# Two broadcast rows spread by TensorE, and the final norm's multiplies shared out over ScalarE and GpSimd

## The chip, the cores and the metric

One core of a Trainium2 chip runs the kernel. The metric is the device time of one execution in microseconds (us). Before the change three runs took 2086.59, 2084.54 and 2086.45 us, median 2086.45 us.

## The reference

The program is a two-layer backbone over 512 latent tokens and 256 context tokens of width 1024, all in float32. Layer 0 mixes by retention and a gated linear recurrence, layer 1 by latent attention, and each layer ends in a mixture of 32 experts of which every token uses two. Only the ends of the two expert parts and the final norm matter here:

```python
def rmsnorm(x, g):
    xf = x.astype(jnp.float32)
    y = xf * lax.rsqrt(jnp.mean(xf * xf, axis=-1, keepdims=True) + EPS)
    return (y * g.astype(jnp.float32)).astype(x.dtype)
...
            # layer 0, after the experts: y is the weighed sum of each token's two expert outputs
            xc = xc + mod_c[5] * y[:b * ctx_len].reshape(b, ctx_len, -1)
            xl = xl + mod_l[5] * y[b * ctx_len:].reshape(b, n, -1)
...
            # layer 1
            xl = xl + mod_l[5] * y.reshape(b, n, -1)
    return rmsnorm(xl, final_norm_g)
```

`mod_l[5]` and `mod_c[5]` are rows of 1024 numbers (the gates), `final_norm_g` is another one. The kernel holds tokens on the 128 partitions, so each such row must stand on all 128 partitions before VectorE can multiply a tile by it.

## The kernel before, in words

A tile is 128 tokens by 1024 channels. The token stream `c.X` stays in SBUF (six tiles, the first two are context), and each expert writes its output rows to the DRAM tensor `ys`. Two stages gather them back and are the ones that change.

**The middle stage** is `combine_into_mla` (six tiles; its tiles and semaphores are named `comb_...`, at about 1073 to 1126 us). SP issues three small loads (`laid`, 20 KB in all), then the two gates, each a DMA that copies one DRAM row of 4 KB to all 128 partitions (512 KB written, line 1138), waits until tile 0's gathers have landed, and issues the load of the next stage's weights `w_in` (line 1619, 2688 KB). GpSimd issues per tile two indirect gathers of 512 KB (line 2469). Tile buffers are three deep, so the gather of tile 3 waits until tile 0 is done. ScalarE scales one of the two gathered rows (`weigh`, 2485). VectorE adds the other (2554), multiplies by the gate (2556), adds to `X` (2557). ScalarE squares and sums the tile and takes the root (159, 162), VectorE inverts it (2527), GpSimd refines the inverse by five instructions on one column (2456 to 2460) and scales the identity with it (2463), and TensorE turns the tile with that matrix (2590).

**The last stage** is `combine` (four tiles, from 2042 us to the end). SP loads one gate, waits for tile 0's gathers, loads the final norm's row in the same way (2631), and stores the finished tiles (2637). GpSimd only issues gathers (2357). ScalarE weighs (2373), squares and takes the root. VectorE does the three operations of each tile (2398, 2400, 2401), then, one tile behind, the inverse with its refinement (lines 95 to 100, six small instructions) and the final product with `1/rms` and the norm's row in one instruction (2646). The constant `eps`, which the root needs and for which the first square waits (line 157 and `eps_set`), is set by VectorE after tile 1, in `prepare` (2641).

The order on each engine is the order in which the program lists the instructions; there is no planner. `Chain` makes each linked instruction of an engine wait for the one before it. SP's queue and GpSimd's are in order as well: what stands behind a waiting instruction waits too. In both stages the DMAs of SP and the gathers of GpSimd go to different queues of the same 16 DMA engines.

Of the kernel before, what the change touches and what calls it, by code (L numbers as in the profile page):

```python
# [14 lines left out]
P = 128  # L15
DM = 1024
# [33 lines left out]
class Chain:  # L50


    def __init__(self, eng, sem, base=0):
        self.eng, self.sem, self.n = eng, sem, base
# [117 lines left out]
class NormModulate(RowNorm):  # L172
# [23 lines left out]
    def load(self, sp):  # L196

        self.load_gains(sp)
        self.load_shift_scale(sp)
# [2121 lines left out]
            more.vector(dve)  # L2321


def combine(nc, c, a, layer, t0, r, prefetch=None):


    T = NT - t0
    with Scope(nc, f"comb{layer}") as s:
        YB = 3
        y = [[s.sb(f"y{b}{k}", [P, DM]) for k in range(2)] for b in range(YB)]  # L2330
        got = [s.sem(f"got{b}") for b in range(YB)]
        weighed, x_done, chain = s.sem("weighed"), s.sem("x_done"), s.sem("chain")
        gate = s.sb("gate", [P, 1 if t0 else 2, DM])
        gate_ready = s.sem("gate_ready")
        gs, ex = s.sb("gs", [P, T]), s.sb("ex", [P, T])
        exp_done, w_done = s.sem("exp_done"), s.sem("w_done")
        tile_done = lambda eng, t: eng.wait_ge(x_done, t + 1)
        norm = FinalNorm(nc, c, a, s, t0, tile_done)
        block = s.block()

        @block.sync
        def _(sp):
            load_gates(sp, c, gate, gate_ready, layer, 1, 1 if t0 else 2)
            sp.wait_ge(got[0], 32)
            norm.load(sp)
            if prefetch:
                prefetch(sp)
            norm.store(sp)

        @block.gpsimd  # L2350
        def _(pool):
            for t in range(T + 1):
                if t < T:
                    if t >= YB:
                        pool.wait_ge(x_done, t - YB + 1)
                    for k in range(2):
                        nc.gpsimd.indirect_dma_start(y[t % YB][k][:], None, c.ys[:, :],  # L2357
                                                     bass.IndirectOffsetOnAxis(r.slot[:, k * T + t:k * T + t + 1], 0)
                                                     ).then_inc(got[t % YB], 16)
                if t >= 3:  # L2360
                    norm.shift(pool, t - 3)
            for t in range(T - 2, T):
                norm.shift(pool, t)

        @block.scalar
        def _(act):
            nc.scalar.activation(r.gshift[:, 0:T, :], r.gshift[:, 0:T, :], ACT.Exp).then_inc(exp_done, 1)
            nc.scalar.activation(ex[:], r.eshift[:, 0:T], ACT.Exp).then_inc(exp_done, 1)
            act.wait_ge(w_done, 1)
            for t in range(T + 2):  # L2370
                if t < T:
                    act.wait_ge(got[t % YB], 32 * (t // YB + 1))
                    nc.scalar.mul(y[t % YB][0][:], y[t % YB][0][:], r.w[:, 0, t:t + 1]).then_inc(weighed, 1)  # L2373
                if 1 <= t <= T:
                    norm.square(act, t - 1)
                if t >= 2:
                    norm.first_half(act, t - 2)
                    norm.second_half(act, t - 2, nc.scalar.copy)

        @block.vector  # L2380
        def _(dve):
            link = Chain(dve, chain)
            V = nc.vector


            dve.wait_ge(exp_done, 2)
# [5 lines left out]
            dve.wait_ge(gate_ready, 16 if t0 else 32)  # L2392
            for t in range(T + 2):
                if t < T:
                    st = 1 if t0 + t < CT else 0
                    y0, y1 = y[t % YB]
                    dve.wait_ge(weighed, t + 1)
                    link(V.scalar_tensor_tensor(out=y0[:], in0=y1[:], scalar=r.w[:, 1, t:t + 1], in1=y0[:],  # L2398
                                                op0=ALU.mult, op1=ALU.add))
                    link(V.tensor_tensor(y0[:], y0[:], gate[:, st, :], ALU.mult))  # L2400
                    V.tensor_tensor(c.X[:, t0 + t, :], c.X[:, t0 + t, :], y0[:], ALU.add).then_inc(x_done, 1)  # L2401
                if t == 1:
                    norm.prepare(dve)
                if 1 <= t <= T:
                    norm.scale(dve, link, t - 1)

        @block.tensor
        def _(pe):
            for t in range(T):
                norm.transpose(pe, t)  # L2410


def combine_into_mla(nc, c, a, r, m):
# [4 lines left out]
    with Scope(nc, f"comb{layer}") as s:  # L2418
        YB = 3
        y = [[s.sb(f"y{b}{k}", [P, DM]) for k in range(2)] for b in range(YB)]  # L2420
        got = [s.sem(f"got{b}") for b in range(YB)]
        gate = s.sb("gate", [P, 2, DM])
        gs, ex = s.sb("gs", [P, T]), s.sb("ex", [P, T])
        turn = [s.sb(f"turn{i}", [P, P]) for i in range(2)]
        laid = s.sb("laid", [5 * KD, P])
# [5 lines left out]
        (gate_ready, weighed, x_done, chain, exp_done, w_done, laid_ready, cols_tr, cols_done, rstd_done, scaled, tr, ev_act,  # L2431
         ev_dve, pchain, inverted, kv_done, kv_out) = (s.sem(n) for n in (
             "gate_ready", "weighed", "x_done", "chain", "exp_done", "w_done", "laid_ready", "cols_tr", "cols_done",
             "rstd_done", "scaled", "tr", "ev_act", "ev_dve", "pchain", "inverted", "kv_done", "kv_out"))
        norm = RowNorm(nc, c, a, s, 0, lambda eng, t: eng.wait_ge(x_done, t + 1), s.sb)
        block = s.block()
# [41 lines left out]
        def _(act):  # L2478
            nc.scalar.activation(r.gshift[:, 0:T, :], r.gshift[:, 0:T, :], ACT.Exp).then_inc(exp_done, 1)
            nc.scalar.activation(ex[:], r.eshift[:, 0:T], ACT.Exp).then_inc(exp_done, 1)  # L2480
            act.wait_ge(w_done, 1)

            def weigh(t):
# [35 lines left out]
        def _(dve):  # L2519
# [97 lines left out]

class Box:
    pass


class FinalNorm(RowNorm):


    def __init__(self, nc, c, a, s, t0, x_ready):
        super().__init__(nc, c, a, s, t0, x_ready, s.sb)
        self.o = s.sb("o", [P, self.T, DM])
        self.o_done, self.stored = s.sem("o_done"), s.sem("stored")

    def load(self, sp):  # L2630
        sp.dma_start(self.g[:], self.a["final_norm_g"].rearrange("(o n) -> o n", o=1)
                     .to_broadcast([P, DM])).then_inc(self.g_ready, 16)

    def store(self, sp):
        for t in range(self.T):
            sp.wait_ge(self.o_done, t + 1)
            sp.dma_start(self.c.out[0, t * P:(t + 1) * P, :], self.o[:, t, :]).then_inc(self.stored, 16)
        sp.wait_ge(self.stored, 16 * self.T)

    def prepare(self, dve):  # L2640
        self.nc.vector.memset(self.eps[:], EPS).then_inc(self.eps_set, 1)
        dve.wait_ge(self.g_ready, 16)

    def scale(self, dve, link, t):
        self.inverse(dve, link, t)
        self.nc.vector.scalar_tensor_tensor(out=self.o[:, t, :], in0=self.c.X[:, self.t0 + t, :],  # L2646
                                            scalar=self.rstd[:, t:t + 1], in1=self.g[:],
                                            op0=ALU.mult, op1=ALU.mult).then_inc(self.o_done, 1)

    def shift(self, pool, t):  # L2650
        pass

    transpose = first_half = shift

    def second_half(self, eng, t, copy):
        pass


def backbone(nc, a, out):
# [71 lines left out]
```

## Time and profile before

| | us |
|---|---|
| median of three runs | 2086.45 |
| the profiled execution, time | 2084.73 |
| its span, first to last instruction | 2083.1 |
| TensorE busy | 1703.4 (82%) |
| VectorE busy | 691.1 (33%) |
| ScalarE busy | 439.0 (21%) |
| GpSimd busy | 257.6 (12%) |

The span is what the trace shows. The 1.6 us between span and time lie before and behind it. A share of busy time is an average over stages with different limits. The chain of waits is followed back from the last instruction only as far as 2042 us, that is over the last stage.

### The profile page before, as it was taken

How to read it: one execution, taken by the hardware profiler on the slowest of the kernel's cores; microseconds unless marked ns; L12 is line 12 of the kernel's file. 1: busy time of each engine (PE TensorE's matmuls, PEld its weight loads, DVE VectorE, ACT ScalarE, POOL GpSimd, SP SyncE). 2: the span in 40 equal slices, each digit the busy share in tenths (PEclk: the TensorE clock that was granted, in tenths of full speed). 3: DMA queues.
4: the chain of work that ended last, by engine and by line, in shares of the span. 5: the costliest groups of instructions: out<-in, count | busy, mean ns of one | idle time of the engine just before them, and what ended most of it. 6: DMA issues, size and time to landing. Idle time of an engine off the chain costs nothing. (4 is left out here: it accounts for less than half of the span.)

```text
span 2083.1 us, 26474 instructions
## 1 busy us (share of the span) xinstructions
PE 1703.4 (82%) x9120; PEld 884.2 (42%) x9121; DVE 691.1 (33%) x1241; ACT 439.0 (21%) x842; POOL 257.6 (12%) x381
## 2 busy tenths in 40 slices
PE   5999999799499789997638999999948899766560
PEld 3443344645245334443316445555534344333330
DVE  3404675733312111111124447775432111111114
ACT  3103454211001100111124125553101101101012
POOL 1002440311101000101013200000121000000001
PEclk9999999899599899999778999999959899877775
DMA  9876744410789999999972102001459999999994
GB/s 371 270 265 222 278 161 153 170 82 31 303 335 398 415 417 409 420 413 407 424 278 91 59 0 92 1 1 50 176 223 394 418 406 414 419 416 424 419 387 148
DMA packets 98212, 560.19 MB, mean 269 GB/s; under 512 B 17188, under 2 KB 35328, under 8 KB 58584
## 3 DMA queue, kind: packets, MB, share of 16 engines
q1 hardware_dynamic: 85104, 522.39, 63.1%
q0 software_dynamic: 7744, 20.98, 3.0%
q10 hardware_dynamic: 5288, 15.80, 2.0%
q8 instruction: 48, 0.79, 0.2%
q14 instruction: 28, 0.23, 0.0%
HBM read 522.88 MB, written 41.50 MB: 271 GB/s over the span
## 5 line engine op out<-in xcount | busy, mean ns | idle before, releaser
L2136 PE MATMUL exp_gps<-moew_wg,all_hT 128*64 128x512 f32 (+1 forms) x480 | 248.3, 643 | 48.2 <-DMA moew_wu<-in_moe_w_up 42.5
L2130 PE MATMUL exp_gps<-moew_wg,all_hT 128*32 128x256 f32 x1088 | 167.5, 475 | 130.9 <-DMA moew_wu<-in_moe_w_up 123.2
L2137 PE MATMUL exp_ups<-moew_wu,all_hT 128*64 128x512 f32 (+1 forms) x480 | 246.1, 638 | 0.0
L588 PE MATMUL abp_ps<-ab_w,all_hT 128*128 128x512 f32 x384 | 169.8, 597 | 0.6 <-PE abp_ps L592 0.3
L2130 PE MATMUL exp_ups<-moew_wu,all_hT 128*32 128x256 f32 x1088 | 166.7, 474 | 1.5 <-issue 1.5
L2130 PEld LDWEIGHTS exp_gps<-moew_wg,all_hT 128*32 128x32 f32 x1088 | 74.5, 135 | 195.7 <-issue 173.8
L2136 PEld LDWEIGHTS exp_gps<-moew_wg,all_hT 128*64 128x64 f32 (+1 forms) x480 | 79.8, 171 | 171.5 <-issue 170.5
L2278 DVE TENSOR_TENSOR all_hT<-all_hT,exp_ups 64x512 f32<-64x512 f32 (+1 forms) x30 | 20.7, 690 | 370.4 <-ACT all_hT L2221 370.4
L2177 PE MATMUL exp_yps<-moew_wd,all_hT 128*64 128x512 f32 (+1 forms) x240 | 115.1, 596 | 0.0
L2179 PE MATMUL exp_yps<-moew_wd,all_hT 128*64 128x512 f32 (+1 forms) x240 | 115.1, 596 | 0.0
L588 PEld LDWEIGHTS abp_ps<-ab_w,all_hT 128*128 128x128 f32 x384 | 71.4, 190 | 99.0 <-issue 97.5
L2276 DVE TENSOR_TENSOR all_hT<-all_hT,exp_ups 64x256 f32<-64x256 f32 x34 | 14.4, 424 | 290.2 <-ACT all_hT L2219 290.2
L2137 PEld LDWEIGHTS exp_ups<-moew_wu,all_hT 128*64 128x64 f32 (+1 forms) x480 | 80.6, 171 | 54.5 <-issue 54.5
L2089 POOL COPY exp_idx<-all_tok 128x1 int32 (+1 forms) x64 | 11.5, 180 | 743.4 <-DVEq L2267 699.8
L1432 PE MATMUL att_sc<-mlakv_KT,mlak_QT 96*128 96x384 f32 x256 | 100.4, 517 | 1.7 <-PEq L76 1.7
L2221 ACT ACTIVATE all_hT<-exp_gps 64x512 f32<-64x512 f32 (+1 forms) x30 | 17.8, 592 | 363.6 <-PE exp_ups L2137 363.6
L592 PE MATMUL abp_ps<-all_hT,ab_w 128*128 128x256 f32 (+1 forms) x256 | 87.8, 500 | 2.0 <-DVE all_hT L745 1.7
L2114 PE MATMUL exp_xps<-all_ident,all_hT 128*128 128x128 f32 x512 | 74.5, 290 | 14.0 <-DMA all_hT<-h_rows,exp_idx 14.0
L2114 PEld LDWEIGHTS exp_xps<-all_ident,all_hT 128*128 128x128 f32 x512 | 64.3, 194 | 47.4 <-issue 47.4
L1504 DVE TENSOR_REDUCE att_nmax<-att_sc 128x1 f32<-128x768 f32 x64 | 61.2, 956 | 49.6 <-PE att_sc L1432 49.6
L2130 PEld LDWEIGHTS exp_ups<-moew_wu,all_hT 128*32 128x32 f32 x1088 | 73.7, 135 | 4.9 <-issue 2.0
L2219 ACT ACTIVATE all_hT<-exp_gps 64x256 f32<-64x256 f32 x34 | 12.8, 375 | 292.3 <-PE exp_ups L2130 292.3
(425 smaller groups left out, 2531.2 us busy)
## 6 DMA issues: line engine op xcount, KB each, us to landing
moew_wg<-in_moe_w_gate SPq DMA_DIRECT2D x64, 2048.0 KB, 29.5
moew_wu<-in_moe_w_up SPq DMA_DIRECT2D x64, 2048.0 KB, 38.2
moew_wd<-in_moe_w_down SPq DMA_DIRECT2D x64, 2048.0 KB, 33.4
all_X<-in_ada_w SPq DMA_DIRECT2D x40, 1024.0 KB, 8.0
ab_w<-in_ab_w_in SPq DMA_DIRECT2D x6, 2048.0 KB, 9.1
ys<-abp_zero SPq DMA_DIRECT2D x32, 384.0 KB, 8.4
ys<-exp_y ACTq DMA_DIRECT2D x13, 512.0 KB, 10.1
ab_rows<-in_ada_w SPq DMA_DIRECT2D x6, 1024.0 KB, 16.1
```

What stands on the lines that cost most here:

```text
L588: last = nc.tensor.matmul(ps[i % RB][:], hT[:, kk, what * P:(what + 1) * P], w[n % S][:, kk, :], start=(kk == 0), stop=(kk == KD - 1))
L592: last = nc.tensor.matmul(ps[i % RB][:, 0:m], w[n % S][:, kk, ct * P:(ct + 1) * P], hT[:, kk, o:o + m], start=(kk == 0), stop=(kk == KD - 1))
L1432: last = nc.tensor.matmul(sc[n % 2][:, b, 0:HALF], k.QT[0:QD, h, t * P:(t + 1) * P], k.KT[0:QD, h, b * HALF:(b + 1) * HALF], start=True, s ...
L1504: V.tensor_reduce(nmax[:, n % R:n % R + 1], sc[n % 2][:, :, 0:HALF], mybir.AxisListType.XY, ALU.max, negate=True).then_inc(mx, 1)
L2114: last = nc.tensor.transpose(xps[k // 4][:, k % 4, :], x_by[q][:, k, :], c.ident[:])
L2130: last = nc.tensor.matmul(bank[lo + j * Q:lo + (j + 1) * Q, 0:HC], x[:, k, 0:Q], wt[:, k, j * HC:(j + 1) * HC], start=(k == 0), stop=(k == ...
L2136: nc.tensor.matmul(gps[0:rows, :], x[:, k, 0:rows], w.g[q][:, k, :], start=(k == 0), stop=(k == KD - 1))
L2137: last = nc.tensor.matmul(ups[at:at + rows, :], x[:, k, 0:rows], w.u[q][:, k, :], start=(k == 0), stop=(k == KD - 1))
L2177: nc.tensor.matmul(yps[0][0:rows, :], hT[:, k, 0:rows], w.d[q][:, k, 0:512], start=(k == 0), stop=(k == HT_N - 1))
L2179: last = nc.tensor.matmul(yps[1][at:at + rows, :], hT[:, k, 0:rows], w.d[q][:, k, 512:1024], start=(k == 0), stop=(k == HT_N - 1))
L2221: nc.scalar.activation(sg[at:at + rows, :], gps[0:rows, :], ACT.Silu).then_inc(sg_done, 1)
L2278: nc.vector.tensor_tensor(h[at:at + rows, :], sg[at:at + rows, :], ups[at:at + rows, :], ALU.mult).then_inc(h_done, 1)
```

## The change

In both stages the gate rows are loaded as they are, 4 KB to one partition. TensorE multiplies a column of ones by that row, four times 512 numbers, which puts the row on all 128 partitions in PSUM. ScalarE copies the first half of each 1024 numbers to SBUF, VectorE the second. In the last stage the second row spread this way is the final norm's. In the middle stage both are gates, and the PSUM banks used are those that later take the turned tiles.

In the last stage the final norm is shared out anew. VectorE sets `eps` first and keeps only the reciprocal. GpSimd refines the inverse behind the last gather. For tiles 0 to 2 ScalarE multiplies the tile by `1/rms`, and GpSimd multiplies it by the norm's row. Tile 3 is finished by VectorE in one instruction as before. `FinalNorm` goes.

```diff
+def load_gate_rows(sp, c, row, ready, layer, sub, streams):
+    for st in range(streams):
+        sp.dma_start(row[0:1, st * DM:(st + 1) * DM],
+                     c.mods[st, layer:layer + 1, (sub * 3 + 2) * DM:(sub * 3 + 3) * DM]).then_inc(ready, 16)
...
 def combine(nc, c, a, layer, t0, r):                                  # last stage
         def _(sp):
-            load_gates(sp, c, gate, gate_ready, layer, 1, 1 if t0 else 2)
-            sp.wait_ge(got[0], 32)
-            norm.load(sp)
+            load_gate_rows(sp, c, row, row_ready, layer, 1, 1)
+            sp.dma_start(row[0:1, DM:], a["final_norm_g"].rearrange("(o n) -> o n", o=1)).then_inc(row_ready, 16)
+            for t in range(T):
+                if t < T - 1:
+                    sp.wait_ge(o_done, t + 1)
+                else:
+                    sp.wait_ge(last_done, 1)
+                sp.dma_start(c.out[0, t * P:(t + 1) * P, :], o[:, t, :]).then_inc(stored, 16)
...
         def _(pool):
+            def refine(t):
+                col = slice(t, t + 1)
+                pool.wait_ge(inverted, t + 1)
+                link(nc.gpsimd.tensor_scalar(ms[:, col], ms[:, col], 1.0 / DM, EPS, ALU.mult, ALU.add))
+                link(nc.gpsimd.tensor_tensor(tmp[:, col], rstd[:, col], rstd[:, col], ALU.mult))
+                link(nc.gpsimd.tensor_tensor(tmp[:, col], tmp[:, col], ms[:, col], ALU.mult))
+                link(nc.gpsimd.tensor_scalar(tmp[:, col], tmp[:, col], -0.5, 1.5, ALU.mult, ALU.add))
+                nc.gpsimd.tensor_tensor(rstd[:, col], rstd[:, col], tmp[:, col], ALU.mult).then_inc(refined, 1)
+            def gained(t):
+                pool.wait_ge(spread_act, 2)
+                pool.wait_ge(spread_dve, 2)
+                pool.wait_ge(scaled, t + 1)
+                nc.gpsimd.tensor_tensor(o[:, t, :], o[:, t, :], gain, ALU.mult).then_inc(o_done, 1)
+            for t in range(T):
                 ...                                                   # all gathers as before
+            for t in range(T):
+                refine(t)
+                if t < T - 1:
+                    gained(t)
...
         def _(act):
+            for i in range(0, 4, 2):
+                act.wait_ge(spread_done, i + 1)
+                nc.scalar.copy(spread[:, i // 2, 0:512], bps[i][:]).then_inc(spread_act, 1)
...
+            def scale(t):
+                act.wait_ge(refined, t + 1)
+                nc.scalar.mul(o[:, t, :], c.X[:, t0 + t, :], rstd[:, t:t + 1]).then_inc(scaled, 1)
+            weigh(0)
+            weigh(1)
+            act.wait_ge(eps_set, 1)
+            for t in range(T):
+                square(t)
+                if t + 2 < T:
+                    weigh(t + 2)
+                if 1 <= t < T:
+                    scale(t - 1)
...
         def _(dve):
+            V.memset(eps[:], EPS).then_inc(eps_set, 1)
...
+            for i in range(1, 4, 2):
+                dve.wait_ge(spread_done, i + 1)
+                V.tensor_copy(spread[:, i // 2, 512:], bps[i][:]).then_inc(spread_dve, 1)
+            dve.wait_ge(spread_act, 2)
+            dve.wait_ge(spread_dve, 2)
+            for t in range(T):
                 ...                                                   # the three operations of a tile as before
+                if t >= 1:
+                    inverse(t - 1)                                    # waits root_done, one reciprocal
+            inverse(T - 1)
+            dve.wait_ge(refined, T)
+            V.scalar_tensor_tensor(out=o[:, T - 1, :], in0=c.X[:, t0 + T - 1, :], scalar=rstd[:, T - 1:T], in1=gain,
+                                   op0=ALU.mult, op1=ALU.mult).then_inc(last_done, 1)
...
         def _(pe):
+            pe.wait_ge(row_ready, 32)
+            for i in range(4):
+                nc.tensor.matmul(bps[i][:], c.ones[0:1, :], row[0:1, i * 512:(i + 1) * 512], start=True, stop=True).then_inc(spread_done, 1)
...
 def combine_into_mla(nc, c, a, r, m):                                 # middle stage
-            load_gates(sp, c, gate, gate_ready, layer, 1, 2)
+            load_gate_rows(sp, c, row, row_ready, layer, 1, 2)
             sp.wait_ge(got[0], 32)
             load_w_in(sp, a, m)
...
+            # ScalarE, behind its two exponentials: banks 0 and 2; VectorE, behind cols: banks 1 and 3
+                nc.scalar.copy(gate[:, i // 2, 0:512], tp[i][:].rearrange("p a b -> p (a b)")).then_inc(spread_act, 1)
+                V.tensor_copy(gate[:, i // 2, 512:], tp[i][:].rearrange("p a b -> p (a b)")).then_inc(spread_dve, 1)
-            dve.wait_ge(gate_ready, 32)
+            dve.wait_ge(spread_act, 2)
+            dve.wait_ge(spread_dve, 2)
...
+            # TensorE, behind the transpose of laid
+            pe.wait_ge(row_ready, 32)
+            for i in range(4):
+                nc.tensor.matmul(tp[i][:].rearrange("p a b -> p (a b)"), c.ones[0:1, :], row[0:1, i * 512:(i + 1) * 512],
+                                 start=True, stop=True).then_inc(spread_done, 1)
```

## Rows read from the trace of the kernel before

**Rows 1.** Page, costliest groups: mean ns of one, then idle time before them.
```profile
L2130 PE MATMUL exp_gps<-moew_wg,all_hT 128*32 128x256 f32 x1088 | 167.5, 475 | 130.9 <-DMA moew_wu<-in_moe_w_up 123.2
```
**Rows 2.** Chain of waits, last stage: start us, us, what.
```profile
2044.39 5.66 DMA comb_y<-ys,all_slot
...
2051.43 1.30 DVE comb_y L2398
...
2055.24 1.21 DVE comb_y L2398
...
2077.51 1.28 DVE comb_o L2646
```
**Rows 3.** Timeline, last stage: start us, us, engine, line, operation.
```profile
2042.40 0.35 SPq L1138 DMA_DIRECT2D comb_gate<-mods  x1
2043.11 0.97 POOL L2357 DMA_INDIRECT comb_y<-ys,all_slot  x1 [70.96 <-PEq L73]
...
2055.51 1.75 POOL L2357 DMA_INDIRECT comb_y<-ys,all_slot  x1 [5.17 <-DVE all_X L2401]
...
2059.01 1.06 ACT L159 ACTIVATE comb_njunk<-all_X 128x1024 f32<-128x1024 f32 x1 [4.46 <-DVE comb_neps L2641]
...
2061.67 1.13 ACT L2373 ACTIVATE comb_y<-comb_y,all_w 128x1024 f32<-128x1024 f32 x1
```
**Rows 4.** Timeline, middle stage.
```profile
1073.61 0.38 SPq L2443 DMA_DIRECT2D comb_laid<-in_norm_g  x1
1074.03 0.82 SPq L1138 DMA_DIRECT2D comb_gate<-mods  x2
...
1075.15 0.33 PE L2569 MATMUL comb_cps<-all_ident,comb_laid 40*128 40x40 f32 x1 [7.11 <-DMA comb_laid<-in_norm_g]
...
1084.54 1.28 DVE L2554 SCALAR_TENSOR_TENSOR comb_y<-comb_y,all_w 128x1024 f32<-128x1024 f32 x1 [8.55 <-ACT comb_y L2485]
...
1097.76 1.15 ACT L2485 ACTIVATE comb_y<-comb_y,all_w 128x1024 f32<-128x1024 f32 x1 [4.16 <-DMA comb_y<-ys,all_slot]
...
1102.26 1.27 DVE L2554 SCALAR_TENSOR_TENSOR comb_y<-comb_y,all_w 128x1024 f32<-128x1024 f32 x1
```
**Rows 5.** Windows from tile 0's first gather to its landing: busy times, TensorE clock, DMA share, GB/s.
```profile
1073.48:1083.17 9.69, 0.33 (x1) 0.18 (x1) 1.14 (x7) 0.88 (x3) 5.71 (x6) 0.50 0.85 274
2043.11:2050.05 6.94, 0.00 (x0) 0.00 (x0) 0.67 (x4) 0.90 (x3) 5.41 (x6) 0.50 0.84 270
```
**Rows 6.** Tile view of the middle stage's gates: us from issue to landing.
```profile
DMA to landing us min/median/max: 5.0/6.6/8.3
```
**Rows 7.** Window of TensorE at half clock, six matmuls of 128x512 (columns as in rows 5).
```profile
560.70:565.80 5.10, 5.10 (x6) 2.13 (x7) 0.00 (x0) 1.00 (x1) 1.04 (x1) 0.50 0.95 382
```
**Rows 8.** Timeline of the same place: two such matmuls, one behind the other.
```profile
562.51 1.92 PE L2137 MATMUL exp_ups<-moew_wu,all_hT 128*128 128x512 f32 x2
```
**Rows 9.** Groups by shape: copies of one PSUM bank, mean ns.
```profile
L2211 ACT COPY all_hT<-exp_xps 128x512 f32<-128x512 f32 x64 | 37.4, 585 | 114.7 <-PE exp_xps L2114 114.7
L2268 DVE COPY all_hT<-exp_xps 128x512 f32<-128x512 f32 x64 | 44.1, 690 | 26.5 <-PE exp_xps L2114 25.8
```
**Rows 10.** Timeline of GpSimd in the middle stage, VectorE busy, then idle.
```profile
1092.22 0.19 POOL L2456 TENSOR_SCALAR comb_nms<-comb_nms 128x1 f32<-128x1 f32 x1 [0.61 <-DVE comb_nrstd L2527]
1092.49 1.11 POOL L2457 TENSOR_TENSOR comb_ntmp<-comb_nrstd 128x1 f32<-128x1 f32 x1
...
1096.20 0.19 POOL L2460 TENSOR_TENSOR comb_nrstd<-comb_nrstd,comb_ntmp 128x1 f32<-128x1 f32 x1
...
1099.60 0.19 POOL L2456 TENSOR_SCALAR comb_nms<-comb_nms 128x1 f32<-128x1 f32 x1
...
1100.70 0.19 POOL L2460 TENSOR_TENSOR comb_nrstd<-comb_nrstd,comb_ntmp 128x1 f32<-128x1 f32 x1
```
**Rows 11.** Timeline, attention's output stage: GpSimd and VectorE at once.
```profile
1466.99 2.35 POOL L277 TENSOR_TENSOR mlak_QT<-mlak_QT 128x1024 f32<-128x1024 f32 x1 [290.11 <-DVE mlak_QT L268]
...
1467.74 2.14 DVE L1132 TENSOR_TENSOR all_X<-all_X,mla_cqT 128x512 f32<-128x512 f32 x1
```

More of the change, by code:

```diff
@@ L2331, in combine @@
         got = [s.sem(f"got{b}") for b in range(YB)]
-        weighed, x_done, chain = s.sem("weighed"), s.sem("x_done"), s.sem("chain")
-        gate = s.sb("gate", [P, 1 if t0 else 2, DM])
-        gate_ready = s.sem("gate_ready")
-        gs, ex = s.sb("gs", [P, T]), s.sb("ex", [P, T])
-        exp_done, w_done = s.sem("exp_done"), s.sem("w_done")
-        tile_done = lambda eng, t: eng.wait_ge(x_done, t + 1)
-        norm = FinalNorm(nc, c, a, s, t0, tile_done)
+        o, junk = s.sb("o", [P, T, DM]), s.sb("junk", [P, DM])
+        row = s.sb("row", [1, 2 * DM])
+        spread = s.sb("spread", [P, 2, DM])
+        gate, gain = spread[:, 0, :], spread[:, 1, :]
+        bps = [s.ps(f"bps{i}", [P, 512]) for i in range(4)]
+        gs, ex = s.sb("gs", [P, T]), s.sb("ex", [P, T])
+        ms, root, rstd, tmp = (s.sb(n, [P, T]) for n in ("ms", "root", "rstd", "tmp"))
+        eps = s.sb("eps", [P, 1])
+        (weighed, x_done, chain, pchain, row_ready, spread_done, spread_act, spread_dve, exp_done, w_done, eps_set, sq, root_done,
+         inverted, refined, scaled, o_done, last_done, stored) = (s.sem(n) for n in (
+             "weighed", "x_done", "chain", "pchain", "row_ready", "spread_done", "spread_act", "spread_dve", "exp_done", "w_done",
+             "eps_set", "sq", "root_done", "inverted", "refined", "scaled", "o_done", "last_done", "stored"))
         block = s.block()
@@ L2350, in _ @@
+            sp.wait_ge(stored, 16 * T)
         @block.gpsimd
         def _(pool):
[L2352 to L2361, printed above, removed]
@@ L2362, in _ @@
-            for t in range(T - 2, T):
-                norm.shift(pool, t)
+            link = Chain(pool, pchain)
+            def refine(t):
[6 more added lines that the diff above has]
+                nc.gpsimd.tensor_tensor(rstd[:, col], rstd[:, col], tmp[:, col], ALU.mult).then_inc(refined, 1)
@@ new lines, in gained @@
+            def gained(t):
[4 more added lines that the diff above has]
+            for t in range(T):
+                if t >= YB:
+                    pool.wait_ge(x_done, t - YB + 1)
+                for k in range(2):
+                    nc.gpsimd.indirect_dma_start(y[t % YB][k][:], None, c.ys[:, :],
+                                                 bass.IndirectOffsetOnAxis(r.slot[:, k * T + t:k * T + t + 1], 0)
+                                                 ).then_inc(got[t % YB], 16)
@@ L2368, in _, with weigh, square @@
             nc.scalar.activation(ex[:], r.eshift[:, 0:T], ACT.Exp).then_inc(exp_done, 1)
+            for i in range(0, 4, 2):
+                act.wait_ge(spread_done, i + 1)
+                nc.scalar.copy(spread[:, i // 2, 0:512], bps[i][:]).then_inc(spread_act, 1)
             act.wait_ge(w_done, 1)
[L2370 to L2378, printed above, removed]
+            def weigh(t):
+                act.wait_ge(got[t % YB], 32 * (t // YB + 1))
+                nc.scalar.mul(y[t % YB][0][:], y[t % YB][0][:], r.w[:, 0, t:t + 1]).then_inc(weighed, 1)
+            def square(t):
+                col = slice(t, t + 1)
+                act.wait_ge(x_done, t + 1)
+                nc.scalar.activation(junk[:], c.X[:, t0 + t, :], ACT.Square, accum_out=ms[:, col]).then_inc(sq, 1)
+                act.wait_ge(sq, t + 1)
+                nc.scalar.activation(root[:, col], ms[:, col], ACT.Sqrt, scale=1.0 / DM, bias=eps[:]).then_inc(root_done, 1)
+            def scale(t):
[10 more added lines that the diff above has]
+                    scale(t - 1)
         @block.vector
@@ L2390, in _ @@
             V.tensor_tensor(r.w[:, 1, 0:T], r.w[:, 0, 0:T], ex[:], ALU.mult).then_inc(w_done, 1)
+            for i in range(1, 4, 2):
+                dve.wait_ge(spread_done, i + 1)
+                V.tensor_copy(spread[:, i // 2, 512:], bps[i][:]).then_inc(spread_dve, 1)
             dve.wait_ge(w_done, 1)
[L2392 to L2405, printed above, removed]
+            dve.wait_ge(spread_act, 2)
+            dve.wait_ge(spread_dve, 2)
+            for t in range(T):
+                y0, y1 = y[t % YB]
+                dve.wait_ge(weighed, t + 1)
+                link(V.scalar_tensor_tensor(out=y0[:], in0=y1[:], scalar=r.w[:, 1, t:t + 1], in1=y0[:],
+                                            op0=ALU.mult, op1=ALU.add))
+                link(V.tensor_tensor(y0[:], y0[:], gate, ALU.mult))
+                V.tensor_tensor(c.X[:, t0 + t, :], c.X[:, t0 + t, :], y0[:], ALU.add).then_inc(x_done, 1)
+                if t >= 1:
[4 more added lines that the diff above has]
+                                   op0=ALU.mult, op1=ALU.mult).then_inc(last_done, 1)
         @block.tensor
         def _(pe):
-            for t in range(T):
-                norm.transpose(pe, t)
+            pe.wait_ge(row_ready, 32)
+            for i in range(4):
+                nc.tensor.matmul(bps[i][:], c.ones[0:1, :], row[0:1, i * 512:(i + 1) * 512], start=True, stop=True).then_inc(spread_done, 1)
 def combine_into_mla(nc, c, a, r, m):
@@ L2422, in combine_into_mla @@
         gate = s.sb("gate", [P, 2, DM])
+        row = s.sb("row", [1, 2 * DM])
         gs, ex = s.sb("gs", [P, T]), s.sb("ex", [P, T])
@@ L2480, in _ @@
             nc.scalar.activation(ex[:], r.eshift[:, 0:T], ACT.Exp).then_inc(exp_done, 1)
+            for i in range(0, 4, 2):
+                act.wait_ge(spread_done, i + 1)
+                nc.scalar.copy(gate[:, i // 2, 0:512], tp[i][:].rearrange("p a b -> p (a b)")).then_inc(spread_act, 1)
             act.wait_ge(w_done, 1)
@@ L2619 @@
     pass
[L2622 to L2656, printed above, removed]
 def backbone(nc, a, out):
```

14 lines of the change are left out of this document (8 added, 6 removed).

## The prediction

> **What bounds the kernel now.** I read the page first. TensorE is busy for most of the span, and its largest group stood idle for 131 us, 123 of them waiting for expert weights [rows 1]. The change touches neither. It touches two short stages between the bulk parts, where everything hangs on the gathers of tile 0. So I read the chain of waits next, then the timeline of each stage. In the last stage the chain goes through the landing of tile 0's gathers (2044.39 + 5.66 = 2050.05 us), then VectorE, which starts at 2051.43 and ends its last instruction at 2078.79 [rows 2]. I call that start S; before, the end is S + 27.4. In the middle stage VectorE starts at 1084.54, 1.37 us after the landing at 1083.17 [rows 4, 5]. All later work of that stage and of the program follows in order from this start, and no transfer of the next part runs ahead of it except `w_in`, so I take a microsecond won there as a microsecond of the program.
>
> **Middle stage, what goes.** Two gates, 2 x 128 rows of 4 KB = 1.05 MB, leave the DMA engines. Up to the landing they moved 274 GB/s x 9.69 us = 2.66 MB, in the last stage, with one gate, 270 x 6.94 = 1.87 MB [rows 5]. Without gates 1.61 MB are left, at 274 GB/s 5.9 us, so tile 0 lands at 1073.48 + 5.9 = 1079.4. That keeps the share of tile 1 that moved along. Bounds: 6.9 us as with one gate (1080.4), and 3.9 us for the 1.05 MB of tile 0 alone (1077.4).
>
> **Middle stage, what comes.** The nearest small load, `laid`'s third, was issued at 1073.61, and TensorE started on it at 1075.15, 1.54 us later. The two row loads stand where the gates stood, so the second goes out at 1074.44 [rows 4] and has landed at 1076.0. The slower bound is 5.0 us, the fastest landing of a gate [rows 6]; I take 1.54, since the bytes (4 KB) are those of that load. TensorE's clock was granted at 0.50 here, its 1.2 GHz level, after tens of us with next to no matmul [rows 5]. At 0.50 a 128x512 matmul takes 0.85 us (5.10 / 6) and the last of a run 1.92 - 0.85 = 1.07 [rows 7, 8]. The four end at 1077.1, 1077.9, 1078.8 and 1079.6. ScalarE copies banks 0 and 2 (0.585 us each) and is free at 1079.4, VectorE banks 1 and 3 (0.69) and is done at 1080.4 [rows 9]. Behind these copies stand ScalarE's `weigh(0)` and VectorE's tile 0. ScalarE is free just when the tile lands, and its scaling covers VectorE's last copy: VectorE starts at 1079.4 + 1.37 = 1080.8. That is **3.8 us** early. If the tile lands sooner ScalarE's copies hold it and nothing more is won; at 1080.4 it is 2.8. The cover is thin: a row landing 1 us later costs 0.6 to 1 us.
>
> The small instructions of GpSimd and the PSUM banks are first needed more than 10 us later, so the spread delays nothing there. `w_in` is issued at the landing and moves with it.
>
> **Last stage, start.** One gate, 0.52 MB, goes, and the norm's row, which competed with tiles 1 and 2. 1.87 - 0.52 = 1.35 MB at 270 GB/s is 5.0 us. The other estimate is tile 3, gathered alone: at most 2061.67 - 2055.51 = 6.2 us, of which 0.8 is its slower first issue (1.75 against 0.97) [rows 3], so 5.4. I take 5.2: landed at 2048.3. The second row load is issued at 2042.75 and lands at 2044.3; the matmuls end from 2045.4 to 2047.9; ScalarE is free at 2047.7, VectorE at 2048.7. Hidden. VectorE starts at 2048.3 + 1.38 = 2049.7, **1.7 us** early. Bounds 0 (nothing comes of the bytes) and 2.4 (ScalarE's copies hold it).
>
> The DMA engines serve both queues at once in these rows. By the Trainium skill, "DMA: Bandwidth & Descriptors", section "SWDGE vs HWDGE vs iDMA", each engine takes turns between the two kinds of queue; a gate would then cost the gathers its own bytes, 1.9 us, where the rows with one and two gates differ by 2.75. By that difference tile 0 would land 0.8 us sooner in the last stage.
>
> **Last stage, the rest,** in us from S. A tile costs VectorE 2055.24 - 2051.43 = 3.8 [rows 2]. What goes is its wait for `eps` and the root (2.9 between tiles 1 and 2), five small refinements and one 1.3 us product per tile, except the last. Left to itself VectorE would be done with tile 3 at about 15.7. So the end is set elsewhere:
> - Tile 0 done 3.8. ScalarE's square, table load, root take 2061.67 - 2059.01 = 2.7 [rows 3]: root at 6.6, `weigh(2)` to 7.8. VectorE ends tile 1 at 7.6, inverts, starts tile 2 at 7.85, ends at 11.65.
> - GpSimd refines tile 0 from 7.9. While VectorE works, one column takes it 1.11 instead of 0.19: from 1092.22 to 1096.39, 4.2 us in all; idle, 1099.60 to 1100.89, 1.3, with the hand-over 1.4 [rows 10]. Refined at 12.05. Meanwhile ScalarE waits for tile 3 (at most 10.3) and weighs it, then scales tile 0 from 12.1 to 13.25 (1.15, as `weigh`).
> - GpSimd's product of 128x1024 took 2.35 us [rows 11]. In that time VectorE's sum of two SBUF tiles, 128x512, took 2.14, where one twice as wide takes 1.30 [rows 2]: it was held until GpSimd was done. So `gained(0)` asks at 13.35, gets the port at 14.45 behind VectorE's product and ends at 16.8; VectorE's last sum for tile 3 stands until then and ends at 17.95; refinement of tile 1 ends at 19.15.
> - From here VectorE is idle and GpSimd and ScalarE take turns, since `gained(t)` stands before `refine(t + 1)` in GpSimd's queue: scale(1) 20.4, gained(1) 22.8, refine(2) 24.2, scale(2) 25.4, gained(2) 27.85, refine(3) 29.25, VectorE's last product 30.6.
>
> 30.6 - 27.4 = **3.2 us** late. The stores are as many and as large as before, the last alone. Bounds: without any holding VectorE ends tile 3 at 15.65, gained(0) ends at 15.7, and the rest of the chain, refine 1.4, scale 1.2, gained 2.4 twice and refine and product, 2.8, ends at 28.5: + 1.1. Upwards, one more VectorE operation in the way of GpSimd: + 4.5.
>
> The row shows the holding. The Trainium skill, "SBUF — State Buffer", section "SBUF: two separate sides", says that a GpSimd operation and a VectorE operation with two SBUF inputs exclude each other for a whole instruction, whoever comes first; that speaks against giving GpSimd wide products beside VectorE. Its absence would be the + 1.1 above.
>
> **Sum.** - 3.8 - 1.7 + 3.2 = - 2.3 us. Against the profiled execution: 2084.73 - 2.3 = 2082.4. That execution was 1.7 below the median of the three runs, whose own spread is 2; taken off the median 2086.45, the forecast is **2084.2 us**. 0.2% is 4.2 us, about what a measurement of this kernel can tell from no change.
>
> **Rivals.**
> - *Both starts at their best and no holding* (faster): - 3.8 - 2.4 + 1.1 = - 5.1, 2081.3 us. For it: the difference of 2.75 us per gate. Against: the held sum [rows 11].
> - *The middle gain is given back* (same): `w_in`, 2.75 MB, now starts 3.8 us sooner and meets the gathers of tiles 1 and 2 still in the queue, so these land late. For it: up to now they had a head start, and tile 3's `weigh` at 1097.76 did wait for DMA. Against: that tile was used only at 1102.26, 3.3 us after it was weighed [rows 4], and 1 MB less is to be moved. Price about 2 us: - 0.3, 2086.2 us.
> - *The rows land late* (slower): one mechanism, the landing of the row loads. If they take 5.0 us [rows 6], the middle stage's second lands at 1079.4, the matmuls end at 1083.1, VectorE's copy at 1083.8, and it starts at about 1084.2, a gain of 0.3. In the last stage the row lands at 2047.8, ScalarE is free at 2051.2, VectorE starts at 2052.5, 1.1 late. With + 3.2 that is + 4.0, with a tail at its upper bound + 5.3: 2090.5 to 2091.8 us. It starts to cost once the rows take over 1.6 us in the middle stage and 2.1 in the last, and with 3.2 in both the change is worth nothing. Against: `laid`'s 1.54.
>
> **How the numbers follow.** Forecast 0.64, its own range - 4 to 0 (2082.4 to 2086.5). At its best 0.14, given back 0.14, rows late 0.06, something else 0.02. The range runs from the best case less 0.8 of scatter to the given-back case plus 1.8: 2080.5 to 2088.0. Faster by over 0.2% needs 4.2 us: the best case and an edge of the forecast, 0.16. Slower by over 0.2%: 0.06. Same: 0.78.
>
> **What would show it.** Right: VectorE's first three-step tile starts 5.9 + 1.4 = 7.3 us after the first gather's issue in the middle stage instead of 11.1, and 6.6 instead of 8.3 in the last; TensorE's four spread matmuls at 0.50 end before the gathers land; a VectorE sum of about 3.5 us for tile 3; last product some 30.6 after S. Wrong: spread matmuls waiting past the landing; tiles 1 or 2 late behind `w_in`; GpSimd's products well off 2.35; or the bulk parts between the stages longer or shorter by over 1 us.

## The result: 0.18% slower, and where

Over 20 runs each, the changed kernel takes 2092.16 us in the median against 2087.97 before; the ratio of the means is 1.0018 with a 95% interval of 1.0010 to 1.0027, that is + 3.8 us (+ 2.1 to + 5.6). The forecast was - 2.3 us, its range ended at 2088.0. Single runs of either kernel scatter over some 10 us (before 2080.7 to 2094.0, changed 2086.5 to 2096.2), so I read the stages in the traces, each counted from its own first gather. Up to the middle stage the two programs are the same, and yet the two profiled executions reach it at 1073.5 and 1078.8 us. So 5.3 of the 10 us between the two spans (2083.1 and 2093.2) lie ahead of the first changed instruction.

**The middle stage after.** The timeline, in the columns of [rows 4]:

```profile
1078.78 0.97 POOL L2529 DMA_INDIRECT comb_y<-ys,all_slot  x1 [70.09 <-POOLq L76]
...
1079.32 0.51 SPq L2327 DMA_DIRECT2D comb_row<-mods  x2
...
1082.21 7.19 PE L2639 MATMUL comb_tp<-comb_row,all_ones 1*128 1x512 f32 x8 [1.58 <-DMA comb_row<-mods]
...
1085.27 0.40 SPq L1619 DMA_DIRECT2D mlakv_V<-in_mla_w_in  x1
...
1089.43 0.69 DVE L2614 COPY comb_gate<-comb_tp 128x512 f32<-128x512 f32 x1 [2.62 <-PE comb_tp L2639]
1090.23 1.28 DVE L2621 SCALAR_TENSOR_TENSOR comb_y<-comb_y,all_w 128x1024 f32<-128x1024 f32 x1
```

`w_in` goes out at the landing of tile 0, 6.5 us after the first gather instead of 9.7 [rows 5]: the gathers gained 3.2 us. VectorE starts 11.45 us after the first gather, 0.4 later than before (11.06). In between stands TensorE: four instructions, **eight** records in the trace, 7.19 us.

**The last stage after.** The chain of waits now goes through TensorE at the start, and through GpSimd and ScalarE in turn to the end; where [rows 2] have the landing of the gathers, it has the spread:

```profile
2050.24 7.20 PE comb_bps L2469 x8
2057.47 0.70 DVE comb_spread L2447
...
2058.39 1.30 DVE comb_y L2454
...
2069.83 1.15 ACT comb_y L2407
2070.98 1.05 ACT comb_o L2418
...
2072.19 2.34 POOL comb_o L2382
...
2077.78 1.16 ACT comb_o L2418
...
2079.09 2.34 POOL comb_o L2382
...
2082.84 1.16 ACT comb_o L2418
...
2084.15 2.34 POOL comb_o L2382
...
2087.89 1.28 DVE comb_o L2462
```

VectorE starts 9.21 us after the first gather (2049.18) instead of 8.32, and from there to the end of its last product is 30.78 us instead of 27.36. The three together: + 0.4 + 0.9 + 3.4 = + 4.7 us, inside the interval. This trace has 1.7 us more inside the middle stage, which come from TensorE's clock and not from the change (see e7 and e8 below).

### The profile page after: what moved, and what is told of

It reads as the page before. It is cut to its first block and busy times, and to the rows that moved or that the text cites. A ratio compares the mean times of both kernels' runs of the same rounds, so it can differ in the third digit from the quotient of the medians.

```text
span 2093.2 us, 26520 instructions
## 1 busy us (share of the span) xinstructions
PE 1715.6 (82%) x9136; PEld 877.1 (42%) x9137; DVE 689.5 (33%) x1222; ACT 444.0 (21%) x849; POOL 273.1 (13%) x404
## 5 line engine op out<-in xcount | busy, mean ns | idle before, releaser
L2094 POOL DMA_INDIRECT all_hT<-h_rows,exp_idx x64 | 62.9, 982 | 92.2 <-issue 92.2
```

The lines of the kernel that those rows point to most:

```text
L2094: nc.gpsimd.indirect_dma_start(xg[q][0:rows, :], None, c.h_rows[:, :], bass.IndirectOffsetOnAxis(idx[q][0:rows, :], 0), bounds_check=TOK - ...
```

## The experiments

For each kernel the starts of VectorE after the stage's first gather, the end of TensorE's last latent matmul in the middle stage likewise, and the tail (VectorE's first three-step operation to its last product), all from the timelines of the profiled executions. There is one trace of each kernel. Where a stage is the same word for word, the traces differ by 0.1 us in the middle start with the spread (11.39 to 11.49), by 0.2 without it (10.84 to 11.06), and by 0.2 in the last start (8.32 to 8.55, 9.20 to 9.36):

| kernel | middle start | middle end | last start | tail | ratio to before (95%) |
|---|---|---|---|---|---|
| before | 11.06 | 63.8 | 8.32 | 27.36 | |
| changed | 11.45 | 65.5 | 9.21 | 30.78 | 1.0018 (1.0010 to 1.0027) |
| e1, half spread | 8.14 | 60.9 | 8.00 | 30.41 | 1.0011 (1.0000 to 1.0021), not comparable |
| e2, spread, old tail | 11.48 | 64.1 | 9.36 | 27.27 | 0.9998 (0.9988 to 1.0008) |
| e3, old rows, new tail | 10.87 | 63.6 | 8.32 | 30.64 | 1.0011 (1.0000 to 1.0023) |
| e4, refine first | 11.49 | 64.2 | 9.28 | 26.99 | 1.0003 (0.9993 to 1.0013) |
| e5, gain after x | 11.39 | 64.1 | 9.20 | 31.35 | one execution |
| e6, early eps | 10.84 | 63.6 | 8.38 | 24.34 | 0.9984 (0.9975 to 0.9994) |
| e7, needed row first | 8.18 | 63.1 | 7.84 | 30.98 | 1.0006 (0.9997 to 1.0015) |
| e8, that and e6 | 8.29 | 62.9 | 8.48 | 24.94 | 0.9977 (0.9965 to 0.9990) |
| e9, e8, gathers apart | 8.04 | 66.8 | 7.99 | 27.35 | one execution |
| e10, old rows, VectorE tail | 10.84 | 65.3 | 8.55 | 22.45 | 0.9977 (0.9966 to 0.9987) |
| e11, spread and VectorE tail | 8.08 | 61.6 | 7.96 | 22.27 | 0.9952 (0.9939 to 0.9965) |

**e1: is it the spread that holds the starts?**

```diff
-nc.tensor.matmul(bps[i][:], c.ones[0:1, :], row[0:1, i * 512:(i + 1) * 512], ...)
+nc.tensor.matmul(bps[i][:, 0:256], c.ones[0:1, :], row[0:1, i * 512:i * 512 + 256], ...)   # both stages
```

> The changed kernel, but each of the four spread matmuls of both stages covers 256 of its 512 numbers; the copies read these twice, so the second half of each row is wrong. Theory (the spread is what holds the starts): at half clock the four matmuls take 3.6 us instead of 7.2, the price that the prediction had put on the whole spread, so VectorE's first operation comes 7.9 us after the first gather's issue in the middle stage (11.45 in the changed kernel, 11.06 before) and about 6.8 in the last (9.21 and 8.32); the tail of the last stage stays at 30.8 us; the time falls by some 6 us against the changed kernel, 2 against the one before. Rival (the gathers land no sooner without the gates): both starts stay within 0.5 us of before, 11 and 8.3.

Its tile view has the records of the matmuls of each stage, minimum, median and maximum in ns:

```profile
L2639 PE MATMUL comb_tp<-comb_row,all_ones x8: 629/629/791, 1080.1 to 1083.3; 1*128 1x256 f32 x8
```

The changed kernel's view has the same eight at twice the width:

```profile
L2639 PE MATMUL comb_tp<-comb_row,all_ones x8: 1056/1056/1215, 1082.2 to 1088.3; 1*128 1x512 f32 x8
```

The spread takes 3.78 us, the middle stage starts at 8.14 and ends 2.9 us sooner than before. So the gathers do land sooner, and the spread was in the way. In the last stage the start is 8.00: only 0.3 better than before, and not the 6.8 expected. There the spread is over 5.0 us after the first gather, and in its timeline ScalarE still waits for the gathers until 6.7:

```profile
2051.76 0.69 DVE L2447 COPY comb_spread<-comb_bps 128x512 f32<-128x512 f32 x1 [1.01 <-PE comb_bps L2469]
2053.45 1.15 ACT L2407 ACTIVATE comb_y<-comb_y,all_w 128x1024 f32<-128x1024 f32 x1 [1.96 <-DMA comb_y<-ys,all_slot]
```

Its time was expected 2 us below before's and came out 2.3 us above (0 to 4.4), where its stages in the table give - 0.2. The likely reason is that wrong gates in layer 0 send tokens to other experts in layer 1, but no run shows that, so e1 counts here for its two stages and not for its total.

**e2 and e3: one half of the change each.** e2 keeps the spread and has VectorE's refinement and products back (`link(V.reciprocal(...))` to the product, `eps` set after tile 1); e3 is the kernel before with the new tail.

> The changed kernel with the old sharing of the final norm: eps set after tile 1, refinement and last product of every tile on VectorE. Theory: starts as in the changed kernel (11.45 and 9.2 us after the first gather's issue), the last stage's tail from VectorE's first operation back from 30.8 to 27.4 us; against before about +1.3 us. Rival (the late start itself stretches the tail, since tile 3's gather comes later relative to the rest): the tail stays above 29.

> The kernel before with only the new sharing of the final norm; all rows are loaded by the broadcast DMAs as before. Theory: starts as before (11.06 and 8.3 us after the first gather's issue), tail 30.8 us instead of 27.4; against before about +3.4 us. Rival (the tail is long only because the late spread shifts ScalarE and GpSimd against VectorE): the tail is at most 28.5, about +1 us.

Both stages and tails came out by the theory: 11.48, 9.36 and 27.27; 10.87, 8.32 and 30.64. By the traces the two halves add up, neither needs the other, and the tail is the dearer one (+ 3.3). The two ratios agree with that (e2 + 1.4 us by its stages, e3 + 3.1), but are too wide to show it alone.

**e5: is it the hold between VectorE and GpSimd?**

```diff
             for t in range(T):
                 refine(t)
+                if t == 0:
+                    pool.wait_ge(x_done, T)
                 if t < T - 1:
                     gained(t)
```

> The changed kernel, but GpSimd's first wide product also waits until VectorE has added tile 3, so the two never hold each other. Theory (the turns of GpSimd and ScalarE behind one another set the end): VectorE's product for tile 3 falls from 3.28 to 1.22 us and tile 3 is ready 2 us sooner, but the tail stays within 0.6 us of 30.8. Rival (the held VectorE is what costs): the tail falls by the 2 us to about 28.7.

In the changed kernel's timeline the first wide product of GpSimd meets VectorE's gate product of tile 3, which takes 3.28 us instead of 1.22:

```profile
2072.19 2.34 POOL L2382 TENSOR_TENSOR comb_o<-comb_o,comb_spread 128x1024 f32<-128x1024 f32 x1 [1.94 <-ACT comb_o L2418]
2072.33 3.28 DVE L2456 TENSOR_TENSOR comb_y<-comb_y,comb_spread 128x1024 f32<-128x1024 f32 x1
```

In e5's timeline the same VectorE product is free, and GpSimd follows:

```profile
2068.79 1.22 DVE L2458 TENSOR_TENSOR comb_y<-comb_y,comb_spread 128x1024 f32<-128x1024 f32 x1
2070.05 1.22 DVE L2459 TENSOR_TENSOR all_X<-all_X,comb_y 128x1024 f32<-128x1024 f32 x1
2071.35 2.34 POOL L2382 TENSOR_TENSOR comb_o<-comb_o,comb_spread 128x1024 f32<-128x1024 f32 x1 [4.35 <-DVE all_X L2459]
```

Tile 3 is done 2.3 us sooner (16.1 instead of 18.5 from VectorE's start), the tail is 31.35. The hold is real, and waiting it out gains nothing: GpSimd's first product now starts 16.2 us after VectorE's start instead of 13.8. What the tail would be if neither engine held the other, no run here shows.

**e4: is it the order in GpSimd's queue?**

```diff
-            for t in range(T):
-                refine(t)
-                if t < T - 1:
-                    gained(t)
+            refine(0)
+            for t in range(1, T):
+                refine(t)
+                gained(t - 1)
```

> The changed kernel; in GpSimd's queue of the last stage the refinement of tile t + 1 stands before the wide product of tile t. Theory (the order in GpSimd's queue makes refinement, ScalarE's scaling and the wide product take turns): ScalarE's scaling of tile 2 and VectorE's last product no longer wait for wide products in front of their refinement; the tail falls from 30.8 to about 27 us, with the starts unchanged (11.45 and 9.2). VectorE's operations are held as before. Rival (GpSimd's total work sets the end, in whatever order): three wide products and four refinements are the same, the tail stays above 29.5.

26.99. With the same instructions, 3.8 us are gone; GpSimd's total work is not the bound. VectorE was still held, in tile 3's sum (3.39 us) and, as its timeline shows, in the last product, behind `gained(2)`:

```profile
2080.51 2.34 POOL L2382 TENSOR_TENSOR comb_o<-comb_o,comb_spread 128x1024 f32<-128x1024 f32 x1
2080.59 3.33 DVE L2462 SCALAR_TENSOR_TENSOR comb_o<-all_X,comb_rstd,comb_spread 128x1024 f32<-128x1024 f32 x1 [3.44 <-POOL comb_rstd L2376]
```

**e6: what was there to win with the smallest edit?**

```diff
 # combine, VectorE, first instruction
+            V.memset(norm.eps[:], EPS).then_inc(norm.eps_set, 1)
 # FinalNorm.prepare
-        self.nc.vector.memset(self.eps[:], EPS).then_inc(self.eps_set, 1)
```

> The kernel before; only eps is set at the start of the last stage instead of after tile 1. Theory: VectorE's wait of 2.9 us for the first root goes and nothing takes its place; the tail falls from 27.4 to 24.5 us, starts as before (11.06 and 8.3); about -2.9 us against before. Rival (tile 3's gather is late next and holds VectorE): 1 to 2 us are given back, tail 26.

24.34: the tail alone is 3.0 us shorter, and the time is 3.3 us (1.3 to 5.2) below before's.

**e7 and e8: the row that is needed first, first.**

```diff
-            for i in range(4):
+            for i in (2, 3, 0, 1):       # middle stage: the context gate first
...
             weigh(0)
             weigh(1)
+            spread_half(3, 0)            # ScalarE's half of the other row; VectorE's stands behind tile 0
```

> The changed kernel; the row that is needed first is spread first (context gate in the middle stage, the gate in the last), and the copies of the other row stand behind the second weighing on ScalarE and behind tile 0 on VectorE. Theory: only 3.6 us of TensorE stand before the first tile, so VectorE starts 7.8 us after the first gather's issue in the middle stage and 8.0 in the last, where now the landing of the gathers holds it; tail 30.7. About -0.5 us against before, -5 against the changed kernel. Rival (the other row's copies hold tile 0 or 1 anyway): the starts are early, but tile 1 starts over 4.5 us behind tile 0.

> The needed row spread first, as in the run beside it, with the old sharing of the final norm and eps set at the start. Theory: the two starts at 7.8 and 8.0 us, the tail 24.5: -3.2 - 0.3 - 2.9 = -6.4 us against before, ratio 0.9969. Rival (the middle stage's gain is given back by late gathers of tiles 2 and 3): tile 5 of the middle stage starts 40.4 us after the first gather as before instead of 37.2, and the total is only about -3 us.

The starts came (8.18 and 7.84), e7's time stayed level with before (1.0006), and e8's fell by 4.8 us (2.1 to 7.3) where 6.4 were expected. e8's last start is 8.48, no better than before's: its gathers landed late, ScalarE started on them 7.2 us after the first. The middle stage's end gained only 0.7 and 0.9 of the 2.8 us. Two things show. VectorE's late copy puts tile 1 at 4.33 instead of 3.7 behind tile 0, as e7's timeline shows:

```profile
1085.19 1.28 DVE L2638 SCALAR_TENSOR_TENSOR comb_y<-comb_y,all_w 128x1024 f32<-128x1024 f32 x1
...
1088.91 0.68 DVE L2624 COPY comb_gate<-comb_tp 128x512 f32<-128x512 f32 x1
...
1089.52 1.27 DVE L2638 SCALAR_TENSOR_TENSOR comb_y<-comb_y,all_w 128x1024 f32<-128x1024 f32 x1
```

And the first group of latent matmuls (eight instructions, sixteen records) took 5.81 us where it took 4.12 before, which moves the rest by 1.7. That is TensorE's clock, and the spread does not decide it: e10, whose middle stage is the old one word for word, has the slow group, while e3 and e6, equally old there, have not; the changed kernel's trace has it, while e2, e4 and e5, with the same middle stage word for word, have not. The first fence is e10's timeline, the second e3's.

```profile
1109.69 5.81 PE L2620 MATMUL comb_kps<-mlakv_V,all_hT 128*128 128x288 f32 x16 [2.89 <-issue]
```

```profile
1108.87 4.12 PE L2617 MATMUL comb_kps<-mlakv_V,all_hT 128*128 128x288 f32 x16 [2.84 <-issue]
```

The changed kernel's own 65.5 holds 1.7 us of it. Windows over that group give the granted clock as the third number from the end, 0.71 in the changed kernel,

```profile
1111.90:1117.80 5.90, 5.85 (x18) 4.41 (x19) 4.92 (x8) 4.75 (x9) 4.22 (x10) 0.71 0.18 67
```

and 1.00, the 2.4 GHz level, before:

```profile
1106.60:1110.80 4.20, 4.15 (x18) 3.34 (x19) 4.13 (x6) 3.29 (x7) 3.36 (x5) 1.00 0.24 91
```

What sets the two kinds of trace apart stands just before the group, in the turnings of tiles 0 and 1. Here is the changed kernel's timeline:

```profile
1102.86 3.74 PE L2661 MATMUL comb_tp<-comb_turn,all_X 128*128 128x128 f32 x16 [13.46 <-POOL comb_turn L2523]
1107.36 2.05 PE L2661 MATMUL comb_tp<-comb_turn,all_X 128*128 128x128 f32 x16 [0.76 <-POOL comb_turn L2523]
1111.95 5.81 PE L2650 MATMUL comb_kps<-mlakv_V,all_hT 128*128 128x288 f32 x16 [2.54 <-issue]
```

The clock had risen to 1.00 before the first turning was over, the second took 2.05 us instead of 3.78, TensorE idled for 2.54 us, and in the group the clock was back at 0.50 from about 1113.2 to 1116.6. In the five traces with the slow group (changed, e7, e8, e10, e11) the first turning takes 3.40 to 3.74 us. In the other eight it takes 3.78 or 3.79, so there the clock rose later, and it stayed at 1.00 through the group. Why it rose sooner in some stays open.

**e9: why does tile 0 land no sooner than 6.5 us?**

```diff
             for t in range(T):
+                if t == 1:
+                    pool.wait_ge(got[0], 32)
```

> The version with the needed row spread first and the old sharing of the norm; GpSimd issues tile 1's and tile 2's gathers only when tile 0 has landed, in both stages. Theory (tile 0's 1 MB lands late, 6.4 to 6.9 us after the first issue, since the gathers behind it take part of the DMA engines): it lands at about 5.3, so ScalarE's first weighing in the last stage starts at 5.4 instead of 7.0, and w_in goes out at 5.3 instead of 6.5. Rival (that time belongs to two gathers of random rows, whatever stands behind them): both stay within 0.3 us of 6.5. Tiles 1 and 2 land late in either case, so the total says nothing.

The rival came true. With nothing behind them, tile 0's gathers land after 6.49 us in the middle stage and ScalarE starts on them at 6.69 in the last, by the timeline:

```profile
2049.73 0.97 POOL L2372 DMA_INDIRECT comb_y<-ys,all_slot  x1 [68.10 <-POOLq L76]
2051.01 0.96 POOL L2372 DMA_INDIRECT comb_y<-ys,all_slot  x1 [0.31 <-issue]
2056.42 1.15 ACT L2389 ACTIVATE comb_y<-comb_y,all_w 128x1024 f32<-128x1024 f32 x1 [2.89 <-DMA comb_y<-ys,all_slot]
```

**e10 and e11: a version that beats both.** GpSimd only refines tiles 0 to 2, ScalarE scales nothing, and VectorE makes the products when its three-step work is over, filling with two of them the time in which ScalarE squares tile 3. e11 adds the spread, the needed row first, the other row's copies both on ScalarE.

```diff
+            for t in range(T - 1):                       # GpSimd, behind the gathers
+                refine(t)
...
+            def finish(t):                               # VectorE
+                if t < T - 1:
+                    dve.wait_ge(refined, t + 1)
+                else:
+                    ...                                  # root_done, refined_rsqrt on VectorE
+                V.scalar_tensor_tensor(out=o[:, t, :], in0=c.X[:, t0 + t, :], scalar=rstd[:, t:t + 1], in1=gain,
+                                       op0=ALU.mult, op1=ALU.mult).then_inc(o_done, 1)
+            for t in (0, 1, 3, 2):
+                finish(t)
```

> The kernel before with only the last stage's norm changed: eps at the start, GpSimd refines tiles 0 to 2 behind the last gather, and VectorE makes all last products, those of tiles 0 and 1 while ScalarE squares tile 3, then tile 3's refinement and product, then tile 2's; ScalarE scales nothing. Theory (what made the new tail long is that ScalarE's and GpSimd's wide operations take turns, not the moving of small ones): tail 22.2 us, starts as before; -5.2 us against before, ratio 0.9975. Rival (GpSimd, blocked by VectorE's wide operations, refines too late): tail 24.5 or more.

> The same last stage with the rows spread by TensorE, the needed one first, and the second row's copies both on ScalarE behind its second weighing. Theory: middle stage starts at 8.2 us, tile 1 follows 3.8 behind tile 0 and the stage ends 2.8 us earlier than before (61.0 instead of 63.8 us after the first gather, if the clock rises as it did there), last stage starts at 8.0, tail 22.2: -2.8 - 0.3 - 5.2 = -8.3 us against before, ratio 0.996. Rival (of the spread's gain nothing arrives behind the middle stage): as the run beside it, ratio 0.9975.

The tails are 22.45 and 22.27. e11 takes 2079.67 us against 2089.67 for the kernel before beside it, ratio 0.9952 (0.9939 to 0.9965). The stages give - 2.2 (middle, with the slow clock in its profile), - 0.4 and - 5.1 = - 7.7 us; the interval runs from - 7.3 to - 12.7. e10, measured beside it with the old rows and the same tail, has a median of 2084.87. So the spread, with only the needed row ahead of tile 0, is worth some 5 us; the stages of the two traces, which both have the slow group, give 3.7 + 0.6 + 0.2 = 4.5. e11 is also the only kernel but e9 in which VectorE waited for tile 2 of the middle stage (0.92 us), since ScalarE's weighing waited for that tile's gathers; whether `w_in`, which was in transfer then, held them up, no run shows.

## Why the prediction was wrong

- **The step that failed is the price of the spread**: "At 0.50 a 128x512 matmul takes 0.85 us (5.10 / 6)". I divided by records. The float32 matmuls of these stages leave two records for each instruction, as the eight for four instructions above show, so one costs 1.7 to 1.8 us and the four 7.2, not 3.6. The timeline of before could have told: tile 0's turning, eight matmuls in the program, stands there as sixteen (only the 40x40 transpose of `laid` leaves one):

```profile
1097.16 3.78 PE L2590 MATMUL comb_tp<-comb_turn,all_X 128*128 128x128 f32 x16 [21.68 <-POOL comb_turn L2463]
```

  e1, which pays about the price I had written down (3.78 us), says how much this is: with it the middle stage is at - 2.9 and the last at - 0.3, with the full price at + 0.4 and + 0.9. So the price moved the two starts by 3.3 and 1.2, together 4.5 of the 7.0 us that lie between the forecast of - 2.3 and the + 4.7 of the stages. What the next two points say is nearly all of the rest, 0.9 and 1.4 us.
- **The gathers' landing in the middle stage** was sized at 5.9 us and measured 6.2 to 6.9 (6.5 in the changed kernel and in e1): 0.6 of the 3.8 were too much. The late rows below make up the rest of the way from - 3.8 to e1's - 2.9.
- **In the last stage** it was sized at 5.2. Where the spread is out of the way, ScalarE starts on the gathers 6.7 us after the first in e1, e9 and e11, 6.6 in e7 and 7.2 in e8, against 7.0 to 7.3 in the traces with the broadcast gate (before, e3, e6, e10). One gate fewer brought some 0.3 us, not 1.7. Bytes over rate was the wrong model, since 0.52 MB fewer should have saved 1.9 by it. Why one gate costs some 0.3 us in the last stage and two cost 3 in the middle (6.5 without, 9.5 to 9.7 with) stays open; e9 only shows that, with no gate in the queues, the 6.5 us do not come from the gathers behind.
- **The tail** was right: 30.6 forecast, 30.78 measured, and the chain to its end is the one written down (turns of 1.4, 1.2 and 2.4 us). That the number fits to 0.2 is in part luck. GpSimd's first product started at 13.8 after S and held VectorE's gate product of tile 3, where I had it start at 14.45 and hold the sum; then refining tile 1 took 3.1 us beside VectorE's sum, where I had 1.3 behind it, so the refinement ended at 19.35 against 19.15. I weighed the hold at 2.1 us (28.5 against 30.6). e5 only shows that letting GpSimd wait for VectorE does not win them, so that weight stays open. What the runs do price is `gained(t)` in front of `refine(t + 1)` (e4, 3.8 us).
- **The rows landed** 1.4 us after the last load's issue in the last stage, as forecast, and 2.6 in the middle instead of 1.54, so that TensorE began 3.4 us after the first gather instead of 2.5. Why they took longer there stays open. It is past the point from which the rival "rows land late" said it would cost, but far from its 5.0: a late spread came, mostly from another cause. "The cover is thin" was the right warning. The measured time is near that rival's 2091.8, with another mechanism. The rival "at its best" did not happen. "Given back" did not either: in e1, whose start came 2.9 us sooner, the whole 2.9 are still there at the stage's end; e11 shows a wait of 0.92 us that may be of that kind.
- **TensorE's clock** was read rightly, 0.50 in both stages, and the spread ran at 0.50. But the time without matmuls ahead of it was some us, not tens: in the middle stage the last expert matmul ended 7.1 us before `laid`'s (the idle time in [rows 4]).
- **The scatter** of the bulk was taken as 2 us from three runs; 20 runs span 13. The median of before moved with them from 2086.45 to 2087.97, so 1.5 us of the distance between 2084.2 and 2092.16 belong to the starting point.

## What to carry to other kernels

Before TensorE is given a job of copying, take the price from the same kind of instruction in the program's text and count how many records one of them leaves. Here a float32 matmul left two, and after an idle stretch each was paid at half clock. The job can still pay if only what is needed first stands ahead of the first tile (e11 against e10). When an engine's queue alternates a small step that others wait for with a wide one that is needed only later, the order can cost more than the work: put the small steps first. And look for the one wait that a misplaced constant causes before sharing out the arithmetic: one moved line (e6) won 3 us where the new sharing lost 3.4.

## What the runs showed of the hardware

- A GpSimd product of two SBUF tiles, 128x1024 float32, takes 2.34 us. A VectorE operation on two SBUF tiles that falls beside it ends 1.1 us after it (3.28, 3.33 us instead of 1.22, 1.28). The Trainium skill, "SBUF — State Buffer", section "SBUF: two separate sides", says that a GpSimd operation which reads SBUF and a VectorE operation with two SBUF inputs exclude each other for a whole instruction. The traces agree with that.
- A small GpSimd operation on one column takes 1.1 to 1.3 us while VectorE runs such operations, 0.2 while it does not.
- Rows of 4 KB loaded to one partition and four matmuls with one row of ones put two rows on 128 partitions in the last stage in 1.4 (landing) + 7.2 (TensorE, two rows) + 0.7 (copy) = 9.3 us, with TensorE's clock at 0.50 in the windows over the spread. The broadcast DMA of 512 KB that stood there before was done by the time the gathers let VectorE start, 8.3 us after the first of them.
- Two gathers of 512 KB, with no broadcast beside them, take 6.5 us from the first issue to landing with nothing behind them (e9), and 6.2 to 6.9 with four more behind them (the traces with a spread, middle stage).
- In five of thirteen traces the clock rose before tile 0's turning was over, and fell back to 0.50 in the latent group that followed 2.4 to 2.9 us of idle time: 5.81 us instead of 4.12.
